# Layer norms of a transformer kernel: the last tile's sum and squares joined on VectorE, the norm's other work cut finer and reordered

## The reference

```python
mod = jax.nn.silu(c) @ w_ada[l] + b_ada[l]
sh1, sc1, g1, sh2, sc2, g2 = jnp.split(mod[:, None, :], 6, axis=-1)
h = x * (1.0 + sc1) + sh1
y = token_mixer(h, ...)                                  # ends with merged @ w_out
x = layer_norm(DEEPNORM_ALPHA * x + g1 * y, ln1_g[l], ln1_b[l])
h = x * (1.0 + sc2) + sh2
y = conv_ffn(h, ...)                                     # ends with (silu(g) * val) @ w_down
x = layer_norm(DEEPNORM_ALPHA * x + g2 * y, ln2_g[l], ln2_b[l])

def layer_norm(x, g, b):
    mu = mean(x); var = mean((x - mu) ** 2)
    return (x - mu) * rsqrt(var + LN_EPS) * g + b
```

## Time and profile before

| | us |
|---|---|
| three runs | 2410.34, 2404.59, 2410.18 (median 2410.18) |
| the profiled execution, whole | 2407.2 |
| its span, first to last instruction | 2404.8 |
| PE busy | 2337.0 (97%) |
| DVE, ACT, POOL busy | 1265.6, 992.3, 995.6 |

### The profile page before, as it was taken

One profiled execution on the slowest core, in us unless ns is written; L12 is line 12 of the kernel. 1 busy time (PEld: TensorE's weight loads), 2 busy tenths in 40 slices (PEclk: granted clock), 3 DMA queues, 4 the chain that ended last, 5 costly groups with the idle time before them and its releaser, 6 DMA issues.

```text
span 2404.8 us, 32261 instructions
## 1 busy us (share of the span) xinstructions
PE 2337.0 (97%) x11392; PEld 1866.7 (78%) x11392; DVE 1265.6 (53%) x2662; ACT 992.3 (41%) x1649; POOL 995.6 (41%) x808
## 2 busy tenths in 40 slices
PE   6999999999999999999999999999999999999988
PEld 4778778878888876887787888887888867778756
DVE  7575675654445356657567434314640163276684
ACT  6444445344343244544534343423142344333463
POOL 3343222454444443423244544444544434454342
PEclk9999999999999999999999999999999999999999
DMA  8532134322226334212442232223232221222210
GB/s 332 214 123 71 61 115 158 123 73 102 93 88 236 106 149 160 97 36 88 144 146 96 88 105 89 88 96 112 88 105 87 102 78 36 87 88 88 88 45 36
DMA packets 51843, 259.54 MB, mean 108 GB/s; under 512 B 6352, under 2 KB 16080, under 8 KB 26128
## 3 DMA queue, kind: packets, MB, share of 16 engines
q1 hardware_dynamic: 50576, 249.63, 29.9%
q0 software_dynamic: 1152, 8.39, 0.8%
HBM read 249.47 MB, written 7.34 MB: 107 GB/s over the span
## 4 chain that ended last, share of the span: by engine, by line
PE 77%; issue 11%; POOL 5%; DVE 4%; ACT 2%; DMA 1%; SPq 0%; POOLq 0%; DVEq 0%; ACTq 0%
PE bank L738 22%; PE bank L740 21%; PE bank L739 21%; POOL w_lo L595 4%; PE bank L986 2%; PE bank L899 1%; PE bank L1225 1%; PE bank L991 1%; PE bank L1028 1%; PE bank L888 1%; PE bank L874 1%; PE bank L929 1%; PE bank L1214 1%; PE bank L1377 1%; DMA ada_early<-w_ada 0%
## 5 line engine op out<-in xcount | busy, mean ns | idle before, releaser
L595 POOL TENSOR_TENSOR w_lo<-w_raw,w_hi 128x512 fp32r<-128x512 f32 (+1 forms) x684 | 873.1, 1308 | 1208.3 <-ACT w_hi L1429 815.6
L738 PE MATMUL bank<-h_hi,w_hi 128*128 128x512 f32 x1616 | 647.0, 400 | 11.5 <-ACT gates_b L1509 5.6
L740 PE MATMUL bank<-h_hi,w_lo 128*128 128x512 f32 x1616 | 631.4, 391 | 0.0
L739 PE MATMUL bank<-h_lo,w_hi 128*128 128x512 f32 x1616 | 629.8, 390 | 0.0
L738 PEld LDWEIGHTS bank<-h_hi,w_hi 128*128 128x128 f32 x1616 | 304.3, 188 | 85.4 <-issue 18.4
L740 PEld LDWEIGHTS bank<-h_hi,w_lo 128*128 128x128 f32 x1616 | 303.7, 188 | 64.9
L739 PEld LDWEIGHTS bank<-h_lo,w_hi 128*128 128x128 f32 x1616 | 304.4, 188 | 58.3 <-issue 0.5
L1429 ACT ACTIVATE w_hi<-w_raw 128x2048 fp32r<-128x2048 f32 (+2 forms) x112 | 197.6, 1764 | 280.5 <-PE bank L740 227.6
L2293 DVE SCALAR_TENSOR_TENSOR cv<-bank,par,cv 128x511 f32<-128x511 f32 (+1 forms) x176 | 131.6, 749 | 213.4 <-ACT cv L1685 200.4
L1434 ACT ACTIVATE w_hi<-w_raw 128x2048 fp32r<-128x2048 f32 x68 | 129.9, 1910 | 125.5 <-PE bank L740 117.0
L1685 ACT ACTIVATE cv<-bank,par 128x512 f32<-128x512 f32 x88 | 68.3, 779 | 233.4 <-PE bank L740 232.1
(11 more groups left out here) (385 smaller groups left out, 3841.1 us busy)
## 6 DMA issues: line engine op xcount, KB each, us to landing
w_raw<-w_stream SPq DMA_DIRECT2D x150, 1024.0 KB, 4.9
w_raw<-w_down SPq DMA_DIRECT2D x32, 704.0 KB, 4.0
ada_mid<-w_ada SPq DMA_DIRECT2D x20, 1024.0 KB, 5.4
ada_last<-w_ada SPq DMA_DIRECT2D x12, 1024.0 KB, 4.9
ada_early<-w_ada POOLq DMA_DIRECT2D x8, 1024.0 KB, 20.8
ada_late<-w_ada SPq DMA_DIRECT2D x8, 1024.0 KB, 6.3
bias_in<-bias_scratch SPq DMA_DIRECT2D x16, 256.0 KB, 3.0
bias_in<-bias_scratch SPq DMA_DIRECT2D x16, 192.0 KB, 2.7
```

The costliest lines, as they stand in the source:

```text
L595: ins = nc.gpsimd.tensor_tensor(w_lo[r][:, part], w_raw[r][:, part], w_hi[r][:, part].bitcast(fp32), ALU.subtract)
L738: nc.tensor.matmul(out, w[0][:, cols], xh, start=first, stop=False)
L739: nc.tensor.matmul(out, w[0][:, cols], xl, start=False, stop=False)
L740: return nc.tensor.matmul(out, w[1][:, cols], xh, start=False, stop=last)
```

## The change

It has seven parts.

1. `norm_early` is gone, and tile 7 of both projections runs through on PE.
2. DVE adds x[7] to `ln_shift` and its square to `ln_mean` (`last_residual`). PE then does one `by_token` of each whole sum, and one product of `ln_shift` into bank 5.
3. The three dummy products ahead of the tail are gone.
4. `ada_group` after tile 5 does one half, four products; the other two halves, eight products (columns 40 to 47), stand after the replication of the reciprocal in place of the five dummy products for `which` = 0. DVE takes them after the norm.
5. For `which` = 0, DVE's taking of the columns and the affine factors stand before residual 6 instead of residual 7.
6. ACT's copy of the high part is cut into four of 128x512, which stand behind `h_hi` of chunks 0 to 3.
7. Chunk 2 is centred by POOL instead of DVE.

The diff, without the dropped semaphore and two changed calls of `norm_tail`:

```diff
...
         pool.wait_ge(var_ready, k + 1)
-        for f in range(3, KD):
+        for f in range(2, KD):
             if f == KD - 1:
...
 
-    def ada_group(first, halves, late, bank):
-        pe.wait_ge(ada_used, 2 * (first + halves))
-        part = first % 12 - 4 if first % 12 else 0
+    def ada_products(part, halves, late, bank):
         for j in range(4 * halves):
...
                                    ones[:, 0:32], start=True, stop=True)
-        ins.then_inc(ada_sum, 1)
+        return ins
+
+    def ada_group(first, halves, late, bank):
+        pe.wait_ge(ada_used, 2 * (first + halves))
+        ada_products(first % 12 - 4 if first % 12 else 0, halves, late, bank).then_inc(ada_sum, 1)
 
...
 
-    def norm_early(l, which):
-        k = 2 * l + which
-        pe.wait_ge(zcsum_ready, k + 1)
-        nc.tensor.matmul(banks[5][:, :], mean_w, ln_shift[:, :], start=True, stop=False)
-        by_token(4, ln_shift)
-        pe.wait_ge(sq_used, KD * k + 7)
-        by_token(3, ln_mean).then_inc(early_done, 1)
-
     def norm_stats(l, which, f):
...
         elif f == 7:
-            pe.wait_ge(tile_evac, tdone(l, t + 6))
-            keep_warm(0, 3)
-            pe.wait_ge(tile_evac, tdone(l, t + 7))
-            by_token(2, x[:, 7, :]).then_inc(tok_done, 1)
-            pe.wait_ge(sq_ready, KD * (k + 1))
-            by_token(7, ln_sq[1]).then_inc(sq_used, 1)
-            nc.tensor.matmul(banks[5][:, :], mean_w, x[:, 7, :], start=False, stop=True).then_inc(rest_done, 1)
+            pe.wait_ge(zcsum_ready, 2 * (k + 1))
+            by_token(2, ln_shift).then_inc(tok_done, 1)
+            pe.wait_ge(sq_used, KD * (k + 1))
+            by_token(7, ln_mean).then_inc(tok_done, 1)
+            nc.tensor.matmul(banks[5][:, :], mean_w, ln_shift[:, :], start=True, stop=True).then_inc(rest_done, 1)
             pe.wait_ge(inv_ready, k + 1)
...
             ins.then_inc(rep_done, 1)
-            keep_warm(0, 5)
+            if which:
+                keep_warm(0, 5)
+            else:
+                pe.wait_ge(ada_used, 2 * (12 * l + 12))
+                ada_products(6, 2, 0, 7).then_inc(ada_sum, 1)
 
...
             wait_bank(l, TILE_OUT + f, (f + 1, 4, 2)[f // 2 - 1])
-            if f < 7:
-                ins = tile(banks[OUT_BANKS[f]][:, :], split(l, SLOT_OUT + f // 2), (f % 2) * D, m_hi, m_lo, KD)
-            else:
-                tile(banks[1][:, :], split(l, SLOT_OUT + 3), D, m_hi, m_lo, 5, last=False)
-                norm_early(l, 0)
-                ins = tile(banks[1][:, :], split(l, SLOT_OUT + 3), D + 5 * P, m_hi, m_lo, 3, 5, first=False)
+            ins = tile(banks[OUT_BANKS[f]][:, :], split(l, SLOT_OUT + f // 2), (f % 2) * D, m_hi, m_lo, KD)
             ins.then_inc(tile_done, 1)
...
                 pe.wait_ge(tile_evac, tdone(l, TILE_OUT + 3))
-                ada_group(12 * l + 9, 3, 0, 6)
+                ada_group(12 * l + 9, 1, 0, 6)
 
...
                     wait_bank(l, TILE_DOWN + f, 2)
-                elif f == 7:
-                    norm_early(l, 1)
                 ins = tile(banks[f % 2][:, :], split(l, SLOT_DOWN + s), 0, u_hi, u_lo, 11, 11 * s, s == 0, s == 1)
...
             split_hi(l, *split_after)
-        for j in ((), (), (), (), (0, 1), (2, 3), (4, 5, 6), (7,))[f]:
+        if f == KD - 1:
+            act.wait_ge(sq_used, k * KD + 6)
+            act.wait_ge(tile_evac, tdone(l, t + 7))
+            A_(ln_sq[1][:, :], x[:, 7, :], ACT.Square).then_inc(sq_ready, 1)
+        for j in ((), (), (), (), (0, 1), (2, 3), (4, 5, 6), ())[f]:
             if j < 4:
...
         A_(ht[0][:, :], banks[5][:, :], ACT.Copy).then_inc(rest_ready, 1)
-        split_hi(l, *split_after)
         act.wait_ge(gb_ready, k + 1)
+        n = slot_no(l, split_after)
+        act.wait_ge(w_full[n % 2], 16 * (n // 2 + 1))
         for j in range(KD):
...
             A_(h_hi[:, j, :], banks[2 + j % 2][:, :], ACT.Identity, bias=ln_gb[:, 8 + j:9 + j]).then_inc(h_hid, 1)
+            if j < 4:
+                part = slice(512 * j, 512 * j + 512)
+                ins = A_(w_hi[n % 2][:, part], w_raw[n % 2][:, part], ACT.Copy)
+                if j == 3:
+                    ins.then_inc(w_hi_done, 1)
         act.wait_ge(h_hid, KD * (k + 2))
...
     def ada_take(l, group):
-        dve.wait_ge(ada_sum, 3 * l + group + 1)
-        cols = (slice(0, 16), slice(16, 36), slice(36, 48))[group]
+        dve.wait_ge(ada_sum, 4 * l + group + 1)
+        cols = (slice(0, 16), slice(16, 36), slice(36, 40))[group]
         n = cols.stop - cols.start
...
 
+    def last_residual(l, which, t):
+        k = 2 * l + which
+        scale = mod[l][:, 23 + 24 * which:24 + 24 * which]
+        dve.wait_ge(tile_done, tdone(l, t + 7))
+        V.scalar_tensor_tensor(x[:, 7, :], banks[1][:, :], scale, x[:, 7, :], ALU.mult, ALU.add).then_inc(tile_evac, 1)
+        dve.wait_ge(tile_evac, tdone(l, t + 7))
+        dve.wait_ge(zcsum_ready, 2 * k + 1)
+        V.tensor_tensor(ln_shift[:, :], x[:, 7, :], ln_shift[:, :], ALU.add).then_inc(zcsum_ready, 1)
+        dve.wait_ge(sq_used, KD * k + 7)
+        dve.wait_ge(sq_ready, KD * (k + 1))
+        V.tensor_tensor(ln_mean[:, :], ln_sq[1][:, :], ln_mean[:, :], ALU.add).then_inc(sq_used, 1)
+
     def residual(l, which, t, f):
...
             dve.wait_ge(x_ready, KD * (k - 1) + f + 1)
-        if f == 7:
-            dve.wait_ge(early_done, k + 1)
-            V.tensor_copy(ln_tok[:, 0:4], per_token(banks[4]))
-            chain(V.tensor_copy(ln_tok[:, 8:12], per_token(banks[3])))
+        if f == KD - 1:
+            last_residual(l, which, t)
+            return
         dve.wait_ge(tile_done, tdone(l, t + f))
...
 
-        dve.wait_ge(tok_done, k + 1)
-        chain(V.tensor_tensor(ln_tok[:, 0:4], per_token(banks[2]), ln_tok[:, 0:4], ALU.add))
+        dve.wait_ge(tok_done, 2 * k + 1)
+        chain(V.tensor_copy(ln_tok[:, 0:4], per_token(banks[2])))
         chain(V.tensor_tensor(ln_tok[:, 0:4], ln_tok[:, 0:4], ln_tok[:, 0:4], ALU.mult))
-        chain(V.tensor_tensor(ln_tok[:, 0:4], ln_tok[:, 0:4], ln_tok[:, 8:12], ALU.subtract))
-        dve.wait_ge(sq_used, KD * (k + 1))
+        dve.wait_ge(tok_done, 2 * k + 2)
         V.tensor_tensor(ln_tok[:, 4:8], per_token(banks[7]), ln_tok[:, 0:4], ALU.subtract).then_inc(var_ready, 1)
...
             if f < KD:
-                if f >= 3:
-                    dve.wait_ge(zs_ready, 5 * k + f - 2)
+                if f >= 2:
+                    dve.wait_ge(zs_ready, 6 * k + f - 1)
                 elif f:
...
         for f in range(KD):
-            if f == 7:
+            if f == 6:
                 ada_take(l, 2)
...
         norm_tail(l, 0)
+        dve.wait_ge(ada_sum, 4 * l + 4)
+        chain(V.tensor_tensor(mod[l][:, 40:48], banks[7][:, 0:256:32], par[l][:, 40:48], ALU.add))
         with dve.Fori(0, KF // 2) as it:
```

More of the change, by code:

```diff
@@ L339, in build @@
         var_ready = sem("var_ready")
-        early_done = sem("early_done")
         tok_done = sem("tok_done")
@@ L1672, in _ @@
                     norm_tile(l, 0, TILE_OUT, f, (SLOT_OUT + f // 2 + 2,) if f % 2 else None)
-                norm_tail(l, 0, (SLOT_OUT + 5,))
+                norm_tail(l, 0, SLOT_OUT + 5)
                 A_(silu_one[:, :], ck[:, C_ONE:C_ONE + 1], ACT.Silu)
@@ L1703, in _ @@
                     norm_tile(l, 1, TILE_DOWN, f, (SLOT_DOWN + 2 * f + 3, cols))
-                norm_tail(l, 1, (SLOT_DOWN + 2 * KD + 1,))
+                norm_tail(l, 1, SLOT_DOWN + 2 * KD + 1)
             def take_h(chunks):
```

## The result

The changed kernel takes 2392.7 us (median of four runs, 2391.9 to 2394.2), the kernel before 2409.8 beside it (four runs, 2404.6 to 2410.3): ratio 0.9935, 95% interval 0.9917 to 0.9952. Forecast were 12.1 us and 2396.0, with a range of 2390 to 2403. The profiled execution took 2393.3 us, its span is 2391.4 (2407.2 and 2404.8 before).

The account below looks back on a forecast made before the run. PE was taken to bound the kernel, its chain covering 77% of the span. The terms -10.2, -1.0, +2.9 and -3.8 gave -12.1 us, from a mean of 2408.1 to 2396.0, range 2390 to 2403.

Parts of the forecast that it names:

- early block out of tile 7: Tile 7 before each norm: PE loses 2.56 us of work with tile work waiting behind it; -10.2 us over four norms.
- column products, norms 0 and 2: After tile 5: four products remain of twelve, but PE waits for residual 4; -0.5 us each, -1.0 us in all.
- additions on the path: Behind residual 7: DVE's addition of x[7] delays `by_token` by 0.72 us, the second addition is hidden; +2.9 us in all.
- end of tail: Normed chunks: `h_hi` starts sooner, POOL centres chunk 2, scaling of chunk 2 comes 0.94 us earlier; -3.8 us in all.
- DVE's 1.84 us in hand: DVE's wait for PE before residual 7, claimed to stay and to cover some 1.2 us of affine work before residual 6.
- The eight products moved into the tail: In norms 0 and 2, 1.73 us replace 1.1 of dummies, ending with the first `h_hi`; cost nothing, uncovered 0.6 us twice.
- both halves: Tail's 0.94 us a norm: quartered weight copy letting `h_hi` start sooner, and chunk 2's centring moved to POOL.
- POOL's sixth subtraction: Before `w_lo` of the next slot: costs 1.25 us, PE comes 0.94 earlier, 1.3 of 3.5 us in hand stay; no cost.
- Additions held up by POOL: Rival, behind residual 7: both additions take 1.76 instead of 0.70 us beside POOL; 7.5 us back, 2403.5; 6%.
- A clock that falls in each norm: Rival: without three dummies PE's 1.65 us wait near residual 7 lowers its clock; at most 6.8 us, 2402.8; 6%.
- a clock that stays low: Rival: the tail's small products don't restore the clock until `first_slot` ends; up to +49 us, 2457; 3%.
- Weights late: Rival: time taken out of tile 7 comes back because the next weights are late; all of it, 2406; 5%.

Follow-up runs that it names:

- e1_filler: Changed kernel with the early block (ones product, two sums by token, results unread) put back into tile 7 of all four norms; 2405.4 us.
- e3_cols_together: Changed kernel with all twelve late column products back at tile 5 and five dummy products in the tail of the first norms; 2393.6 us.
- e4_hi_whole: Changed kernel with the next slot's weight rounding as one 128x2048 piece before the first `h_hi`; 2396.9 us.
- e5_centre_dve: Changed kernel with chunk 2 centred on DVE again, five chunks on POOL instead of six; 2393.1 us.
- e2_no_adds: Changed kernel without the two DVE additions behind residual 7, so norms are computed from seven chunks; 2392.8 us.
- e6_warm: Changed kernel with three dummy products back in PE's gap between tile 7 and the first sum by token; 2396.1 us.
- first comparison: Changed kernel against the kernel before, four runs each: 2392.7 against 2409.8 us, 15.8 us between the means.
- second comparison: Changed kernel run again without edit, against the kernel before in a later group: 2393.3 us, 12.9 us less by the means.
- x10: Changed kernel with seven-chunk sums by token taken in PE's gap, chunk 7 added in the accumulator, the DVE addition of the sums moved later; 2391.0 us.
- x11: Changed kernel with x10's edit and all late column products 128 columns wide; 2391.5 us.
- c0_again: Changed kernel without any edit, rerun as the yardstick beside the follow-up kernels; 2393.3 us.

## Why the prediction was right

By its own steps, with what the rows and runs gave:

| step | forecast us | measured us |
|---|---|---|
| early block out of tile 7 | -10.2 | -10.7 (4 x 2.67, e1_filler) |
| column products, norms 0 and 2 | -1.0 | -0.8 (2 x 0.40, e3_cols_together) |
| additions on the path | +2.9 | +2.9 (4 x 0.72, start of the sum by token, R + 0.81 to R + 1.53) |
| end of tail | -3.8 | -3.9 (4 x 0.98, e4_hi_whole, e5_centre_dve) |
| sum | -12.1 | -12.5 |

*The early block* went off the path whole. DVE's 1.84 us in hand before residual 7 are 1.61 now, so nothing else is late. *The columns* gave 0.1 less each: tile 6 starts at 464.06, where 463.95 was forecast; residual 4 itself comes at 463.16. The eight products moved into the tail cost nothing, as forecast: they end at 482.64, `h_hi` of chunk 0 at 482.61. *The additions* take 0.69 us each in all four norms. Against before they cost what was forecast, 0.72 us a norm (R + 0.81 to R + 1.53). Taking them out of the changed kernel (e2_no_adds) gives only 0.63, since its sum by token then starts at R + 0.89: it waits for another signal than before's. That is the price of the additions within the new kernel, not their share in the change. *The end of the tail* came in both halves. The whole tail, from residual 7 to the last `h_lo`, is 0.25 us shorter, which is these two terms together (0.72 - 0.98); forecast was 0.22.

*POOL's sixth subtraction*: six take 7.52 us, `w_lo` ends at 488.68 + 5.04 = 493.72, PE begins that slot at 494.98 without a wait. That leaves 1.26 us of the 1.3 forecast.

```profile
481.20 7.52 POOL L615 TENSOR_TENSOR x<-x,ht 128x512 f32<-128x512 f32 x6 [11.66 <-ACT ht L1543]
488.68 5.04 POOL L594 TENSOR_TENSOR w_lo<-w_raw,w_hi 128x512 fp32r<-128x512 f32 x4
```

The rivals. *Additions held up by POOL*: they aren't, at 0.69 us. The same kind of addition still takes 1.76 us while POOL subtracts:

```profile
465.39 1.76 DVE L2108 TENSOR_TENSOR bank<-x 128x512 f32<-128x512 f32 x1
```

The Trainium skill ("SBUF — State Buffer", section "Who interferes with whom") says that such an addition, with both inputs in SBUF, contends with GpSimd's reads; these rows agree, with 1.76 us beside POOL's `w_lo` and 0.69 where POOL is idle. It is idle behind residual 7 in all four norms; in norm 1 it ends at 842.38 + 5.03 = 847.41 and the first addition starts at 848.66. *A clock that falls in each norm*, *a clock that stays low*: 1.00 in all four tails, and the gap of 1.64 us does no harm (e6_warm). *Weights late*: no wait. None of the four happened.

What the forecast didn't have is the clock elsewhere. The first comparison came out 3.7 us above the sum. Between the two profiles the falls account for 1.6 us (13.4 with them, 11.8 without), and the second comparison gave 12.9 us with the same kernels. So each part is confirmed by rows to 0.5 us. That the sum of 12.1 lies so near the profiles' 11.8 is in part luck: the parts came out 0.4 larger, and 0.9 us that no part has was given back further on (below). The run times alone leave room for a gain anywhere from 10 to 20 us. Over all nine runs of the changed kernel the mean is 2393.3 us, 2.7 under the forecast of 2396.0, of which 1.5 is the level before: 2406.6 us in the second comparison, 2408.1 in the forecast. The rest is within the scatter.

One thing stays open: three times the shift shrinks where nothing was edited, from -8.15 to -7.80 at about 1075 us, from -14.15 to -13.88 behind 1964, both among small VectorE instructions, and from -13.88 to -13.58 at 2150 to 2190. That is 0.9 us together, which the forecast doesn't have and the table's -12.5 doesn't hold. The first of these stretches, from the start of `h_lo` of chunk 7 in norm 1 to the column products in front of norm 2, has two lengths in the fourteen profiles: 398.5 us in before, e2, e3, e5, x10 and x11, and 398.85 in the changed kernel, c0_again and the six others. What decides between them wasn't tested.

## What to carry to other kernels

Work that stands in the middle of dense TensorE work costs its full length even if all others have time in hand; a VectorE addition that makes one operand out of two is worth its 0.7 us if it saves products there. Find how much of a removed piece a second wait takes back (here 1.3 of 1.7 us, the wait for residual 4) before counting it. And where executions scatter by several us, compare one edit by distances from a common event in each profile: 0.15 us could be read this way where the times could not tell 2. Read them up to the place of the edit and a little beyond: a stretch further on can be longer or shorter by 0.35 us for a reason of its own.

## What the runs showed of the hardware

- Rows of 32-column products let TensorE's granted clock fall to 1.2 GHz although PE is busy without a break: 48 of them took 15.07 us and the low clock lasted from about 833 to 847 us. The same products with 128 columns took 10.88 us at 2.4 GHz, since at the full clock a pass costs 0.11 us either way. A wider product is nearly free here (32 passes took 3.73 us against 3.65), and takes the fall away. What the clock goes by is not shown.
- Falls are not the same in two executions of one program: the one at about 830 us is in seven of eleven profiles with narrow products. Lasting 3.4 us it costs 1.6 to 1.8 us, lasting 6.8 us (e2_no_adds) 3.3. Falls are a part of the 3 us by which the runs scatter: in c0_again the runs with a mean granted clock of 0.996 and 0.998 took 2397.0 and 2391.1 us, but three others at 0.997 took from 2391.4 to 2395.7.
- The two places where the change puts eight passes before a wait, and sixteen in the tail, show a fall in one profile each (e2_no_adds at 464, e4_hi_whole at 482). Whether the narrow products or the waits behind them bring it there isn't shown.
- A VectorE addition of 128x512 with both inputs in SBUF takes 0.69 us with POOL idle and 1.76 us beside POOL's subtractions.
